# A two-layer hybrid trunk in fp32 on one core: GpSimd forms the sums of fetched activations, ScalarE copies two late banks, and a block transpose stands three VectorE operations later

## The reference

```
h = h + fox_mixer(rmsnorm(h, ...), ...)          # layer 0: attention of 16 heads
h = h + sqrelu_mlp(rmsnorm(h, ...), up, down)    # 2048 -> 8192 -> 2048
h = h + retention_mixer(rmsnorm(h, ...), ...)    # layer 1: 8 heads, chunks of 128
h = h + sqrelu_mlp(rmsnorm(h, ...), up, down)
return rmsnorm(h, final_norm)

def sqrelu_mlp(h, w_up, w_down):
    return jnp.square(jax.nn.relu(h @ w_up)) @ w_down
```

## Time and profile before

| | |
|---|---|
| median of three runs | 2564.88 us (2563.68 to 2568.09) |
| profiled execution, its own time | 2560.97 us |
| span from its first to its last instruction | 2559.2 us |
| TensorE busy | 2489.9 us, 97% |
| VectorE busy | 1962.1 us, 77% |
| ScalarE busy | 1446.4 us, 57% |
| GpSimd busy | 165.1 us, 6% |
| mean granted TensorE clock | 0.99 |

### The profile page before, as it was taken

One profiled execution on the slowest core, in us unless ns is written; L12 is line 12 of the kernel. 1 busy time (PEld: TensorE's weight loads), 2 busy tenths in 40 slices (PEclk: granted clock), 3 DMA queues, 4 the chain that ended last, 5 costly groups with the idle time before them and its releaser, 6 DMA issues. The chain is left out here.

```text
span 2559.2 us, 29454 instructions
## 1 busy us (share of the span) xinstructions
PE 2489.9 (97%) x11035; PEld 2045.9 (80%) x11035; DVE 1962.1 (77%) x2007; ACT 1446.4 (57%) x1694; POOL 165.1 (6%) x284
## 2 busy tenths in 40 slices
PE   9999999999999999989999999999999999999998
PEld 8888888788788787768888888888777887878876
DVE  6454556888787888867778867778888888788877
ACT  7454544656555656545556446556565556565654
POOL 0000000000100001101111001101100010010010
PEclk9999999999999999999999999999999999999999
DMA  8454556575757565756665666666576666657574
GB/s 311 150 176 149 172 174 226 189 256 193 231 182 259 187 244 196 248 168 206 214 220 184 233 187 216 199 201 224 206 247 217 221 213 202 228 194 258 179 237 163
DMA packets 133940, 534.79 MB, mean 209 GB/s; under 512 B 17200, under 2 KB 17456, under 8 KB 133424
## 3 DMA queue, kind: packets, MB, share of 16 engines
q1 hardware_dynamic: 115776, 476.65, 54.1%
q0 software_dynamic: 17888, 56.12, 7.3%
q10 hardware_dynamic: 144, 0.26, 0.0%
HBM read 506.74 MB, written 26.21 MB: 208 GB/s over the span
## 5 line engine op out<-in xcount | busy, mean ns | idle before, releaser
L1530 ACT ACTIVATE w_hi<-work 128x1024 fp32r<-128x1024 f32 (+2 forms) x847 | 960.6, 1154 | 718.8 <-DMA work<-in_w_wide 172.3
L2152 DVE TENSOR_TENSOR w_lo<-work,w_hi 128x1024 fp32r<-128x1024 f32 (+2 forms) x847 | 1117.0, 1348 | 323.8 <-ACT w_hi L1530 320.5
L1047 PE MATMUL acc<-w_hi,xT_hi 128*128 128x512 f32 x811 | 319.0, 393 | 7.9 <-DVE xT_lo L2218 3.9
L1049 PE MATMUL acc<-w_hi,xT_lo 128*128 128x512 f32 x811 | 317.4, 391 | 0.0
L1048 PE MATMUL acc<-w_lo,xT_hi 128*128 128x512 f32 x811 | 317.2, 391 | 0.0
L1047 PE MATMUL sc<-w_hi,xT_hi 128*128 128x512 f32 x676 | 264.1, 391 | 0.0
L1049 PE MATMUL sc<-w_hi,xT_lo 128*128 128x512 f32 x676 | 263.2, 389 | 0.0
L1048 PE MATMUL sc<-w_lo,xT_hi 128*128 128x512 f32 x676 | 263.0, 389 | 0.0
L1047 PE MATMUL acc<-w_hi,aT_hi 128*128 128x512 f32 x584 | 232.1, 397 | 11.2 <-DVE aT_lo L2218 5.5
L1915 DVE TENSOR_TENSOR w_lo<-work,w_hi 128x1024 fp32r<-128x1024 f32 x127 | 151.7, 1223 | 103.2 <-ACT w_hi L1322 100.9
L1048 PE MATMUL acc<-w_lo,aT_hi 128*128 128x512 f32 x584 | 229.3, 393 | 0.0
(11 more groups left out here) (321 smaller groups left out, 3887.6 us busy)
## 6 DMA issues: line engine op xcount, KB each, us to landing
work<-in_w_stream SPq DMA_DIRECT2D x400, 512.0 KB, 4.6
work<-in_w_wide SPq DMA_DIRECT2D x212, 768.0 KB, 6.6
work<-in_w_wide SPq DMA_DIRECT2D x178, 512.0 KB, 5.9
park<-stage POOLq DMA_DIRECT2D x38, 512.0 KB, 4.1
evac<-park POOLq DMA_DIRECT2D x152, 128.0 KB, 4.2
qk_park<-evac POOLq DMA_DIRECT2D x8, 512.0 KB, 6.0
work<-qk_park POOLq DMA_DIRECT2D x32, 128.0 KB, 5.4
h<-in_x SPq DMA_DIRECT2D x2, 1024.0 KB, 8.7
```

The source lines that it names most:

```text
L1047: pe.matmul(bank[:, :], x_hi, w_hi[:, c], start=start, stop=False, skip_group_check=True)
L1049: return pe.matmul(bank[:, :], x_lo, w_hi[:, c], start=False, stop=stop, skip_group_check=True)
L1530: ins = act.activation(w_hi[:, ring_cols(place, n)], src[:, first * NB:(first + n) * NB], ACT.Copy)
L2152: ins = dve.tensor_tensor(w_lo[:, c], src[:, first * NB:(first + n) * NB], w_hi[:, c].bitcast(F32), ALU.subtract)
```

## The change

Four things are done.

1. The sums S1 to S4 of fetched blocks are formed on GpSimd's queue, right behind the fetch that they read, and no more on VectorE (16 calls in up pairs, 3 around the retention layer, 4 operations each). GpSimd waits for its own first and second operation, and at the end for the last one, before it goes on to the next turn.
2. In down pairs whose predecessor is a down pair, and in the up pair behind those (i = 3, 4, 7, 8, 11, 12), ScalarE copies the banks e and w of the pair before into tr (`copy_out`), and VectorE adds them to h from tr behind tiles 7 and 8 (`add_copy`), in place of `add_bank` from the banks.
3. In pairs that follow an up pair and in the first pair of the second MLP, `turn_blocks(turn)` stands behind `tau2` and no more behind `tau1`. With it, `relu_squared(0)` of bank e stands behind `seed_u` and no more ahead of it.
4. Around the retention layer: `turn_lo` and `turn_hi` of one turn, `s_low` and `s_high` stand some tiles earlier, one `turn_lo` later behind the adds, and the squares for the norm of a late pair later on ScalarE.

```diff
@@ GpSimd
+            def turned_sums(n, count, first, j, sign):
+                w = width_of_sum(count)
...
+                pool.wait_ge(fetched, GRID * 16 * (n + 1))
+                wait(pool, s_lo, count - 1)
+                small_step(pool.tensor_tensor(s[S1], a21, a22, ALU.subtract))
+                if sign > 0:
+                    small_step(pool.tensor_tensor(s[S2], a11, s[S1], ALU.subtract))
+                else:
+                    small_step(pool.tensor_tensor(s[S2], s[S1], a11, ALU.subtract))
+                pool.tensor_tensor(s[S3], a11, a21, ALU.subtract)
+                pool.tensor_tensor(s[S4], a12, s[S2], ALU.subtract if sign > 0 else ALU.add).then_inc(s_made, 1)
+                pool.wait_ge(s_made, parts_of_sums(count - 1) + (2 if first else 1))
@@ GpSimd, end of turn(n)
+                for m in range(2):
+                    chunk, quad = divmod(n - UPS_AT[m], QUADS)
+                    if 0 <= chunk < SUPER and quad < 2:
+                        turned_sums(n, UNITS[mlp_unit(m, 4 * chunk + 2)].sums, quad * 2 * P, 2 - quad, -1)
+                if n == RET_NORM_AT:
+                    turned_sums(n, X_SUMS_OF_RET, 0, 2, 1)
+                if n in (MLP_NORM_AT, MLP_NORM_AT + 1):
+                    turned_sums(n, X_SUMS_OF_MLP, (n - MLP_NORM_AT) * 2 * P, 2 - (n - MLP_NORM_AT), -1)
@@ ScalarE
+            def copy_out(tok, done, bank, out, count, n):
+                act.wait_ge(done, count)
+                act.wait_ge(turned, n)
+                wait(act, copy_added[tok], T(f"copy{tok}"))
+                act.activation(tr[tok], bank[:, :], ACT.Copy).then_inc(out, 1)
...
                     relu(0, e_done, sc[0], e_out, done, turn + 1)
                     relu(1, w_done, sc[1], w_out, done, turn + 1)
+                if copies:
+                    turns = UPS_AT[m] + (i + 1) // 4 * QUADS
+                    copy_out(0, e_done, sc[0], e_out, done, turns)
+                    copy_out(1, w_done, sc[1], w_out, done, turns)
+                seed_u(u, RET_HEADS * m)
+                if was_up:
                     relu_squared(0, e_out, done)
-                seed_u(u, RET_HEADS * m)
@@ VectorE, wide_pair
-                if turn is not None and not was_plain and not late_norm:
-                    turn_blocks(turn)
                 tau3(u)
                 lo(u, W_TAU1)
                 tau2(u)
+                if turn is not None and not was_plain and not late_norm:
+                    turn_blocks(turn)
...
-                if not was_up:
+                if was_normed:
                     add_bank(0, p_quad + 1, sc[0], e_done, e_out, done, scaled=not by_pe)
...
                 lo(u, 7)
+                if copies:
+                    add_copy(0, p_quad + 1, e_out, done)
                 lo(u, 8)
+                if copies:
+                    add_copy(1, p_quad + 1, w_out, done)
                 if turn is not None and not late_norm:
-                    if new_sums:
-                        wide_sums(turn, 0)
                     turn_lo(turn, *dst, p_quad)
```

71 lines of the change are left out of this document (35 added, 36 removed).

## The result

The changed kernel has a median of 2573.51 us (2563.51 to 2580.49, 20 runs), and the kernel before, run beside it on the same chip, 2564.45 us (2559.15 to 2571.99, 20 runs). The ratio is 1.0027, with a 95% interval of 1.0015 to 1.004. The change made the kernel slower, by 0.15 to 0.4%. The forecast was 2557.8 us, with a range of 2546 to 2570; the closest rival is "GpSimd waits in its turn", at 2573.7 us.

A forecast was written before the change was run, and what follows sets the result against it. TensorE bounds the kernel, waiting ahead of TAU2 on a chain of VectorE, transfers and ScalarE. Terms -13.1 - 1.2 - 3.1 + 5.6 + 4.2 + 0.5 = -7.1 us took 2564.9 to 2557.8 us; range 2546 to 2570.

The forecast's parts named there:

- GpSimd waits in its turn: Rival, GpSimd's sums: each waits for a whole VectorE operation; 2573.7 us, 0.34% slower; chance 0.17.
- the short sums: Second turn, S1 to S4 on GpSimd: `s_high` 0.7 us later, eight times, +5.6 us; 1.9 each if the last `lo` intervenes.
- the trip of the second turn: Second turn's transposes to its last fetch's landing: no term charged; longer fetches considered only in the rival "The waits only move".
- the moves: Transpose and square leave the chain to TAU2: 1.64 us in eight pairs, -13.1; pair 0 of the second MLP, -1.2.
- the copies: Copied banks e and w: five of seven TensorE waits for `seed_w` go, gain 3.1 us, at worst nothing.
- on this the cost is nothing: First turn, park and fetch some 5 us later: 12 us left for a trip needing some 10, so no cost.
- So the gain of the move is near nothing: Sums taken off VectorE: the time freed there was time nobody waited for, so near no gain.
- the long sums: First turn, sums on GpSimd delay VectorE toward `seed_w` by 0.6 us in seven groups, +4.2 us; bounds 0 and 1.5 each.
- The sums cost nothing: Rival: GpSimd's operations fall in VectorE's idle time; 2548 us, or 2544 with clock gains; chance 0.25.
- The waits only move: Rival: parks and loads meet, slower fetches return TAU2's gain as waits at tiles 9 and 13; 2564.4 to 2570.9 us; chance 0.18.
- The signs: TensorE's wait ahead of TAU2: 3.8 us in pair 6; forecast wrong if such waits fall to 2.5 or exceed 5.
- The other sign: GpSimd's sums: the prediction is wrong if they take far more than 0.7 and 0.4 us each.

The follow-up runs named there:

- f1: Changed kernel with the last weight load of the eight sum-forming pairs held until GpSimd has issued the second turn's fetches; 2524.7 us, 1.9% off the changed kernel.
- f3: Kernel before with the last weight load of the eight sum-forming pairs held behind the second turn's fetches; 2527.2 us, 1.45% off the kernel before.
- e1: Changed kernel with the sums of fetched activations back on VectorE at their old places; ratio 0.9968 to the kernel before.
- e3: Kernel before with only the first block transposes and the square of bank e moved; 0.15% faster than the kernel before.
- e6: Kernel before with only the square of bank e moved behind the seed copy on ScalarE; 0.02 to 0.3% slower.
- e10: Changed kernel with the square of bank e ahead of the seed copy again; 0.3% slower than the changed kernel.
- e9: Changed kernel with the short sums back on VectorE, the long ones still on GpSimd; ratio 0.9979 to the kernel before.
- e4: Kernel before with only the copies of banks e and w to tr by ScalarE, added later by VectorE; 0.2% faster.
- e2: Kernel before with only the sums moved to GpSimd; 1.3% slower than the kernel before.
- e7: Kernel before, VectorE still forming all sums, GpSimd forming the same four again into words nobody reads; 1.07% slower than the kernel before.
- f2: Kernel before with transposes moved, copies, seed copy ahead of relus and square in late pairs, and the last weight load held; 2517.83 us, ratio 0.9813.

## Why the prediction was wrong

The forecast was 7.1 us faster, the measured time is 7 (by the ratio) to 9 us (by the medians) slower. Two steps failed: the price of the short sums, which was in the sum with 0.7 us a pair and measured 1.8, and the trip of the second turn, which was taken as unchanged and became 1.7 us longer in the mean of eight pairs. The other terms were right in kind.

The direct terms, read again in the traces, are: the moves 12.6 us (1.6 us from `s_high` to `seed_u` in each of eight pairs) and 1.3 us in pair 0 of the second MLP, the copies 5.3 us, the short sums 8 x 1.77 = 14.2 us against them, and the long ones 2.4 us (0.34 us in each of seven pairs that form sums). That is -2.6 us. The longer trips are 13.7 us more over the eight, and the sum +11.1; the spans of the two traced executions are 12.6 us apart, and the trip of the kernel before was read in an execution 3.5 us below its median, so it may be somewhat short. Two comparisons support this split. With the load held in both, the trips are as short as each other's (13.4 and 13.0 us), and the changed kernel is 2.5 us below the one before (f1 and f3, with overlapping intervals), as the direct terms have it. And e1, which differs from the changed kernel by the sums and has the same trips, is 15 us (by the ratios) to 18 us (by the medians) faster, where 14.2 and 2.4 make 16.6.

**The trip, the step that was missing.** The forecast followed the moved first turn and found that "on this the cost is nothing", which is right: it has room. It did not ask what the same moves do in the pairs that form sums, and of the sums it said "What VectorE is freed of, it did in time that nobody waited for ... So the gain of the move is near nothing." Both change when the loads and the second turn's transfers run beside each other. The moves alone have trips of 18.6 us and gave 4 us in place of 14 (e3); the square alone has 19.0 (e6). In the other direction VectorE, without the long sums, comes up to 1.6 us earlier to the `lo` that frees the last load's buffer. Either seems to be enough for long trips (e1, e10), so the changed kernel's 1.7 us cannot be put down to one of them. That transfers beside the fetches are what makes the trip long is shown by f1 to f3; how the square and the freed buffer bring them together is read from the traces, one execution each.

**The short sums** (+5.6 us). The step that failed is the estimate of 0.7 us, which let S3 and S4 share the time with `turn_lo` alone. The bound that the text gave, 1.9 us if the last `lo` gets in as well, nearly came true: 1.77 us in each of eight pairs, 14.2 us. `lo` had started at 661.90, and S4 was queued 0.36 us later. Undone in e9 they give back 12 to 16 us. This bound was left out of the forecast's own range: with it and the 1.5 for the long sums the range would end at the 2573.7 of the rival and not at 2567, and with nothing for both it would start at 2548 and not at 2547.

**The moves** (-13.1 and -1.2 us). Right in the chain, for the transposes in the time too: alone they gave 0.57%, some 14 us, where 10.6 were forecast for them. Wrong for the square: "leaves the chain too. Together 1.64 us in each of eight pairs" was read in a late pair, and the same line acts in the pairs that form sums, where `seed_u` waits for TensorE and the square was free. In a kernel with its sums on VectorE the park takes longer with it, and so does the trip (e6, e3, and e1's 18.8 us). In the changed kernel, whose trips are long without it, undoing the square's move costs 0.3%, which fits its 0.47 us in eight late pairs (e10).

**The copies** (-3.1 us). Right in kind, and a little small: 5 us in e4, 5.3 in the six pairs of the trace, and six of seven waits for `seed_w` are gone.

**The long sums** (+4.2 us). 2.4 us in the pairs of the trace, 3 us in e9 against e1 with overlapping intervals: right in kind, bar the trip. The text has the block transpose read PSUM as `seed_w` does; it reads tr, which is in SBUF, but as it turned out the fourth sum and the transposes run side by side without loss (0.74 and 1.24 us). The park was issued 0.57 us behind the transposes' end, 0.3 later than before. That they cost so little goes with the moved transposes. In the kernel before, where the first turn lands 5 us earlier and the sums meet three `lo`, the sums cost 34 us in all, and 26 by their presence alone (e2, e7). Of this 10 us are in the pairs that form sums, in both traces, and 25 and 21 in the late pairs. How the latter split between the lock, the trip and the clock was not tried.

**The rivals.** "GpSimd waits in its turn" had the mechanism for the short sums, nearly their size (1.9) and the time (2573.7); that the time fits so well is partly chance, as its long sums were charged at 1.5 us each and cost a third of that or less, and the trips, which it does not have, fill the difference. "The sums cost nothing" is excluded by e7. "The waits only move" had the right suspicion, that loads and transfers of the turns meet. The first turn's trip stayed at 8.2 to 8.8 us (once 9.5) in spite of starting 5 us later, and the second's became longer by about what the rival charged (13.7 us over the eight, against 8 x 1.64 = 13.1). It looked for the price ahead of tiles 9 and 13, where the waits for `turn_lo` fell from 5.5 to 4.3 us; it came ahead of TAU1 and TAU2. Its argument against itself, that "this chain starts from TAU3, and moves with it", leaves out the loads: their start hangs on `lo`, not on TAU3.

**The signs.** The forecast named a wait of 3.8 us ahead of TAU2 in pair 6, and one of 2.5 as the sign that the sums are free. It was 2.1 there, and the sums were anything but free: part of the wait had moved to TAU1, 2.6 us of it. The other sign was the good one: sums that take far more than 0.7 and 0.4 us (up to 2.19 and 1.50).

**What the profile of before had and the forecast did not use.** The eight second trips were not one duration. They took 15.1 to 18.2 us, three below 16.0 and five above 17.3. With the load held, the changed kernel and the one before are hardly to be told apart (f1 and f3, 2524.7 and 2527.2 us, intervals overlapping), while holding it gave 49 and 34 us.

The best kernel is f2, 2517.83 us, 0.9813 of the time before [0.9787, 0.9840].

## What to carry to other kernels

When instructions are moved or an engine is relieved, ask which buffers are freed earlier or later and which transfers then run beside one another; here a transfer on the path that sets the end was worth ordering ahead of the bulk loads by a wait, and not by luck. When one duration of a transfer shows two clusters in a trace, look at what is issued just ahead of it and just behind it in each: one semaphore here was worth more than the whole change. An instruction moved in a loop body moves in every iteration, so its price is to be read in one iteration of each kind.

## What the runs showed of the hardware

**GpSimd beside VectorE.** A GpSimd sum of 128x128 took 0.46 us with VectorE idle and 1.44 to 1.50 when a VectorE instruction of SBUF operands was in front of it, ending 0.3 us behind it; and three `lo` took 5.12 instead of 3.50 us beside GpSimd's. The Trainium skill ("SBUF — State Buffer", section "SBUF: two separate sides") gives the exclusive lock, and the traces agree. They show besides how it goes on when both engines have instructions queued: S3 ended 0.3 us behind `turn_lo`, the `lo` that had come next took 1.48 us where the mean is 1.23, and S4 ended 0.3 us behind that. In pair 5 of the changed kernel the fourth long sum, 128x256, ran beside VectorE's block transposes and took 0.74 us, and the transposes took their 1.24 as before.

**Loads beside a fetch.** Four fetches took 5.4 us in f1, with no load issued from 4.4 us ahead of the first of them to 2.5 us behind it, and 10.5 us in the changed kernel, with loads issued 2.8 and 1.7 us ahead of it, one with it and one 3.3 us behind.

**The clock.** A late pair with waits of 2.1 and 2.6 us ran at a mean granted clock of 0.93, and at 1.00 with waits of 1.3 us in all; the difference in TensorE's own time was 2.8 us. Over the whole span the mean was 0.988 and 0.997.
